# Landing x in three parts in another order: columns 0 to 511 of each row block first, the rest of both together

## What is computed

```python
h = rmsnorm(x, g_mix)                      # per row over 1024 columns
proj = einsum('bsd,de->bse', h, w_in)      # 1024 -> 4256
qa, ka, va, cq, ckv, kr, gate_a, gate_b = split(proj)
# rope, two attentions (8 heads each) over 256 rows, up-projections of cq and ckv
x = x + einsum(g_a * (o_a @ w_o_a) + g_b * (o_b @ w_o_b), w_out)
u = relu(rmsnorm(x, g_mlp) @ w_ff1)        # 1024 -> 4096
x = x + (u * u) @ w_ff2                    # 4096 -> 1024
return rmsnorm(x, g_final)
```

## Time and profile before

| | us |
|---|---|
| median of 3 runs | 364.59 |
| lowest, highest | 364.46, 365.83 |
| the profiled execution's own time | 364.77 |
| its span (first to last instruction) | 363.0 |

### The profile page before, as it was taken

The page is one execution under the profiler, slowest core; times in us unless marked ns, Lnnn a source line. Parts: engine busy times, 40 slices in busy tenths (PEclk is TensorE's granted clock), DMA queues, the critical chain, the costliest instruction groups (busy, mean ns, idle before and its releaser), DMA issues.

```text
span 363.0 us, 5565 instructions
## 1 busy us (share of the span) xinstructions
PE 356.1 (98%) x2109; PEld 310.9 (86%) x2109; DVE 287.4 (79%) x404; ACT 231.8 (64%) x384; POOL 40.9 (11%) x62
## 2 busy tenths in 40 slices
PE   8999999999999999999999999999999999999993
PEld 7998889887788888888888899999999999999983
DVE  4877973958877777487587879999998888998584
ACT  5996436987565675064466657777677777665424
POOL 1341000000000100000021011111101111220002
PEclk9999999999999999999999999999999999999999
DMA  8999567665341366328165999999999998963003
GB/s 263 382 388 311 221 187 239 214 225 166 134 142 38 106 233 228 116 89 325 51 212 168 273 334 221 279 301 293 287 267 268 278 280 248 294 171 116 2 0 116
DMA packets 42198, 76.77 MB, mean 212 GB/s; under 512 B 1924, under 2 KB 19345, under 8 KB 41921
## 3 DMA queue, kind: packets, MB, share of 16 engines
q1 hardware_dynamic: 37840, 66.59, 53.6%
q0 software_dynamic: 4176, 9.64, 13.4%
q10 hardware_dynamic: 160, 0.27, 0.2%
HBM read 75.44 MB, written 1.05 MB: 211 GB/s over the span
## 4 chain that ended last, share of the span: by engine, by line
PE 96%; DMA 1%; DVE 1%; ACT 0%; issue 0%; POOLq 0%; DVEq 0%; SPq 0%; POOL 0%; ACTq 0%
PE ps L1413 29%; PE ps L1415 29%; PE ps L1414 29%; PE ps L1420 4%; PE ps L1611 2%; PE ps L1636 2%; DMA raw<-in_w_in_dram 1%; ACT prob L560 0%; PE ps L1498 0%; PE ps L1527 0%; PE ps L1522 0%; PE ps L1532 0%; DVE xs L1172 0%; POOLq L129 0%; DVE qkT_b L1403 0%
## 5 line engine op out<-in xcount | busy, mean ns | idle before, releaser
L544 ACT ACTIVATE whi<-raw 128x1024 fp32r<-128x1024 f32 (+3 forms) x127 | 119.6, 989 | 14.7 <-PE ps L1415 13.4
L944 DVE TENSOR_TENSOR wlo<-raw,whi 128x1024 fp32r<-128x1024 f32 (+2 forms) x64 | 69.9, 1127 | 25.4 <-ACT whi L544 25.3
L1413 PE MATMUL ps<-whi,xT_hi 128*128 128x512 f32 (+2 forms) x188 | 73.4, 390 | 0.0
L1415 PE MATMUL ps<-whi,xT_lo 128*128 128x512 f32 (+2 forms) x188 | 71.3, 379 | 0.0
L1414 PE MATMUL ps<-wlo,xT_hi 128*128 128x512 f32 (+2 forms) x188 | 71.2, 378 | 0.0
L1415 PE MATMUL ps<-xT_hi,wlo 128*128 128x256 f32 x224 | 63.4, 283 | 0.0
L1414 PE MATMUL ps<-xT_lo,whi 128*128 128x256 f32 x224 | 63.4, 283 | 0.0
L1413 PE MATMUL ps<-xT_hi,whi 128*128 128x256 f32 x224 | 63.3, 283 | 0.0
L1413 PE MATMUL ps<-whi,lat_hi 128*128 128x512 f32 (+2 forms) x134 | 51.7, 385 | 0.0
L1414 PE MATMUL ps<-wlo,lat_hi 128*128 128x512 f32 (+2 forms) x134 | 51.2, 382 | 0.0
L1415 PE MATMUL ps<-whi,lat_lo 128*128 128x512 f32 (+2 forms) x134 | 51.1, 382 | 0.0
(11 more groups left out here) (157 smaller groups left out, 499.9 us busy)
## 6 DMA issues: line engine op xcount, KB each, us to landing
raw<-in_w_ff_dram SPq DMA_DIRECT2D x32, 1024.0 KB, 7.2
raw<-in_w_in_dram SPq DMA_DIRECT2D x14, 1024.0 KB, 6.3
raw<-in_w_out_dram SPq DMA_DIRECT2D x4, 1024.0 KB, 5.1
t_raw<-in_w_ff_dram SPq DMA_DIRECT2D x12, 256.0 KB, 7.9
raw<-in_w_ff_dram POOLq DMA_DIRECT2D x12, 256.0 KB, 4.8
t_raw<-in_w_ff_dram POOLq DMA_DIRECT2D x12, 256.0 KB, 7.2
gates<-in_b_gate_dram POOLq DMA_DIRECT2D x2, 1024.0 KB, 6.8
raw<-in_w_o_a_dram SPq DMA_DIRECT2D x2, 1024.0 KB, 5.1
```

What stands on the lines that cost most here:

```text
L544: return nc.scalar.activation(dst, src, ACT.Copy, scale=scale)
L944: nc.vector.tensor_tensor(wlo[:, s, h * w:(h + 1) * w], raw[:, s, h * w:(h + 1) * w], whi[:, s, h * w:(h + 1) * w].bitcast(F32), ALU.subtr ...
L1413: nc.tensor.matmul(dst, a_hi, b_hi, start=start, stop=False)
L1415: return nc.tensor.matmul(dst, a_lo, b_hi, start=False, stop=stop)
```

## The change

Three things are changed. Part 0 of x is row block 0's columns 0 to 511 (256 KB) and no longer all of that block (512 KB). Part 1 is row block 1's columns 0 to 511 as before, and part 2 is columns 512 to 1023 of both row blocks in one load (512 KB), where it was row block 1's alone. SP issues the parts at the same places of its queue. TensorE's eight transpositions of tiles 4 to 7 all stand behind the wait for part 2, in pairs (0, k), (1, k), and `first_rows(1, 0)` and `first_rows(1, 1)` stand ahead of that wait instead of behind it. The products of zeros at the start are 18 and 5 in number, not 22 and 7.

```diff
-WARM_UP = (22, 7)
+WARM_UP = (18, 5)
 REWARM = 4
-X_PARTS = ((0, 0, KT), (1, 0, 4), (1, 4, KT))
+X_PARTS = ((0, 1, 0, 4), (1, 2, 0, 4), (0, 2, 4, KT))
...
             def load_x(i):
-                t, cols = X_PARTS[i][0], slice(X_PARTS[i][1] * P, X_PARTS[i][2] * P)
-                sp.dma_start(xs[:, t, cols], x_v[:, t, cols]).then_inc(x_landed[i], 16)
+                t0, t1, k0, k1 = X_PARTS[i]
+                cols = slice(k0 * P, k1 * P)
+                sp.dma_start(xs[:, t0:t1, cols], x_v[:, t0:t1, cols]).then_inc(x_landed[i], 16)
...
             for k in range(4):
                 turn_x(0, k).then_inc(x_turned, 1)
-            turn_x(0, 4)
-            turn_x(0, 5)
...
             x_lows(2)
-            turn_x(0, 6)
-            turn_x(0, 7)
             w_lows(2)
...
             x_lows(3)
             w_lows(3)
+            first_rows(1, 0)
+            first_rows(1, 1)
             pe.wait_ge(x_landed[2], 16)
             for k in range(4, KT):
+                turn_x(0, k)
                 turn_x(1, k).then_inc(x_turned, 1)
-            for k in range(4):
-                first_rows(1, k)
+            first_rows(1, 2)
+            first_rows(1, 3)
             for k in range(4, KT):
                 pe.wait_ge(xT_lo_done, len(TURNED) + k - 3)
                 proj(CQ, k)
```

## The result

| | before | with the change |
|---|---|---|
| median | 364.57 us (18 runs, 364.21 to 365.88) | 365.68 us (18 runs, 365.30 to 366.20) |
| ratio | 1 | 1.0029, 95% interval 1.0021 to 1.0036 |
| profiled execution: time, span | 364.77, 363.0 us | 365.85, 364.0 us |
| k tile 4 of the first projection starts | 11.77 us | 12.74 us |

The kernel is 1.06 us slower by the ratio (0.77 to 1.31): clear of noise, and inside the 0.5% that the prediction called no change. Its time, 365.68, lies in the stated range (363.8 to 365.7) by 0.02 us, and outside the 364.3 to 365.0 that the prediction held likeliest.

What follows compares the result with a forecast made beforehand. TensorE, busy 98% of the span, bounds the kernel, with loads ahead of its gapless stream. Landings -0.70, moved turns +0.44, gap +0.35 make +0.09, a late chain +0.16 in all: 364.59 to 364.75 us, range 363.8 to 365.7.

Steps and rivals of the forecast that it cites:

- the sum of +0.16 us: Start of k tile 4: TensorE's own sum +0.09 us, but tile 4's chain ends 0.08 later, +0.16 in all.
- what the prediction gave 0.60: The main forecast for the whole kernel: 364.3 to 365.0 us around 364.75, chance 0.60.
- Its own sign of being wrong: Start of the first 288-column matmul, forecast 16.1 us; over 16.5 either the landings or the clock are wrong.
- 262 KB less ahead, so landings 0.70 us sooner: Head of the load queue: part 0, weight tiles and part 1 land about 0.70 us sooner, part 2 as before.
- The moved transpositions, +0.44: Turns (0,4) to (0,7) behind part 2 stand in a gapless TensorE stream: 4 x 0.11 = +0.44 us.
- The gap of 0.35 us ahead of the second row block's first product: TensorE idles 0.35 us awaiting row block 1 tile 0's low part, a wait the four turns filled before.
- What is late next: Chain from turn (1,4) at 10.04 through high part, weight copy and low part releases tile 4's matmul at 11.93.
- The residue of 0.08 us: At k tile 4, the wait for weight 4's low part ends 0.08 us behind TensorE's own sum.
- 18 and 5 products: Six fewer products of zeros at the start: worth nothing alone, since weight tile 0's load hides it.
- The landings stay: Rival: slow loads at the start are tied to time, not data; +0.45 to +0.86 us, 365.0 to 365.45, chance 0.15.
- Half clock: Rival: TensorE stays at 1.2 GHz beyond the wait for part 2; +2.0 us, 366.6, chance 0.05.
- The gain arrives: Rival: weights land still earlier or the 0.35 us gap is absent; 364.1 us, chance 0.20.

Runs made afterwards that it cites:

- e1: Kernel before with only the products of zeros changed, 18 and 5 in place of 22 and 7: 364.59 us, +0.11 (-0.36 to 0.58).
- e4: Changed kernel with the three loads of x as before, so TensorE's order and 18 and 5 products alone: 366.20 us, +1.75 against before (1.17 to 2.33).
- e7: Kernel before with only transpositions (0,4) to (0,7) moved behind the wait for the last part of x: 364.85 us, +0.55 (0.22 to 0.88).
- e8: Kernel before with only first_rows(1, 0) and (1, 1) moved ahead of the wait for the last part of x: 365.56 us, +1.17 (0.77 to 1.60).
- e2: Changed kernel with 22 and 7 products of zeros as before: 365.80 us, +1.28 against the kernel before (0.84 to 1.68).
- e3: Changed kernel with all four first_rows behind the eight transpositions: 366.13 us, +1.60 against the kernel before (1.02 to 2.19).
- E9: Kernel before with part 0 of x loaded as two half rows back to back, weights behind both: 364.93 us in one run.
- e11: Kernel before with part 0 of x loaded as two half rows back to back, timed over several runs: 365.32 us, +0.87 (0.51 to 1.24).
- e6: Kernel before with SP waiting for the masks before its first load, so all loads come 1.58 us later: 366.79 us in one run.

## Why the prediction was right, and where it was wrong

It forecast no change that a measurement tells, at 364.75 and up to 365.7. The time is 365.68, and the ratio's interval lies wholly above 1. That it falls in the range at all is luck: the sum of +0.16 us was off by 0.9, and what the prediction gave 0.60 did not happen. Its own sign of being wrong came true: the first matmul of 288 columns stands at 17.01, over the 16.5 from which "either the landings or the clock are" wrong. It was the landings.

*262 KB less ahead, so landings 0.70 us sooner.* This is the step that failed. It held for part 0 (0.7) and weight tiles 0 and 1 (0.5 each: 2.9 and 3.6 us from issue, 3.4 and 4.1 before), and for nothing behind them: tile 2 came 4.66 us after its issue, where the earlier trace rows have 4.6. And part 2, which I left in place because the bytes ahead of its end are the same, came 0.7 later. Several profiles say the same (us from issue to landing, issues at the same times):

| loads | tile 0 | tile 1 | tile 2 | tile 3 | part 1 | part 2 |
|---|---|---|---|---|---|---|
| as before (before, e1, e4, e7, e8) | 3.4 to 3.5 | 3.7 to 4.1 | 3.8 to 4.6 | 3.9 to 4.7 | 4.2 to 4.9 | 4.4 to 5.1 |
| of the change (change, e2, e3) | 2.9 | 3.5 to 3.6 | 3.6 to 4.7 | 4.7 to 4.8 | 4.9 to 5.0 | 5.8 to 6.5 |

The first transposition of row block 1 stands at 7.92 to 8.43 in the first five and at 8.35 to 8.41 in the other three, where the prediction had 7.73. Nor was tile 2 what the stretch up to 8 us waited for in the kernel before: the chain shows 0.06 us there.

Why, is argued and not shown. I had counted bytes and not how they are cut. The table of runs orders by it: with 512 KB of x in half rows 335 to 346 GB/s (five profiles), with 1024 KB 291 to 321 (six), with none 348 (one, hardly more than 346). The change doubles the half rows, at the head of the queue. The three profiles with its loads have as many loads as before, issued at the same times, so there the pace is lower without a further load; but they also have another order of bytes. E9 and e11 keep the order and add a load. The cut itself is cheap in a usual packet: at the start of every trace that has them, a packet of half a row of x took 84 ns at the median, and one of a whole row 159. The rest is in slow packets, of up to 1.9 us (e2). Whether they go with the size of the pieces, the places in memory that they skip, the order or the further load, no run here separates.

The prediction also prices the half at 0.60 us by a fit. The Trainium skill, DMA: Bandwidth & Descriptors, Anatomy of one DMA, states that fit for loads that GpSimd issues. These are issued by SP.

*The moved transpositions, +0.44.* Right: e7 measures +0.55 (0.22 to 0.88).

*The gap of 0.35 us ahead of the second row block's first product.* Right in place and size. TensorE had nothing between 9.19, when w_lows gives way (9.02 + 0.17), and 9.52: 0.33 us.

*What is late next.* Right: the chain from turn (1,4) ends last. I priced it at 1.89 us (10.04 to 11.93) and it took 1.93. It came 0.77 late as a whole, since its beginning at 10.04 counted on landings that were not sooner. The residue of 0.08 us by which it ends behind TensorE's own sum was 0.12. What I missed is that it, and not the gap, prices first_rows ahead of the wait: 0.35 by the gap, +1.17 (0.77 to 1.60) measured in e8.

*The terms don't add, and need not.* From the start of the fourth w_lows to k tile 4 the profiles have 2.73 us before, 3.15 in e7, 3.59 in e8, 3.70 in e4 and 3.72 in the change: +0.42, +0.86, +0.97 and +0.99. Both edits together cost 0.97 and not 1.28. In e8 TensorE waits at the end of the chain. In e4 and the change the moved turns fill that wait, and only the one ahead of turn (1,4) delays the chain, by its 0.11. By the medians e7 and e8 give 0.55 + 1.17 = 1.72 and e4 1.75, but e4's median lies between two groups of runs, and the intervals are too wide to tell. So the change loses what its order costs, 0.99, and gains nothing at the landings. Whether the sooner first load gives back a little is open.

*18 and 5 products.* Right: worth nothing that these runs tell (e1, up to 0.58; e2).

*The rivals.* "The landings stay" was priced at +0.45 to +0.86 and given 0.15. It is what happened, by its place in the chain. Its price was short by 0.1: by the profiles the change is 0.97 slower, 0.07 for a turn (1,4) still later than 10.04 + 0.70, and 0.04 for the chain. Its reason is doubtful: I had put slow loads down to the time since launch, and e6 speaks rather against that. "Half clock" was right in what it said of the level, and its price didn't come. With the change the four transpositions from 3.72 us start 0.21 us apart, twice the 0.11 of the earlier trace rows, so TensorE was at 1.2 GHz there, having run 18 and 5 products since 0.98 us, while the granted clock reads 1.00. The Trainium skill, TensorE: Matmul & The Clock Gate, What's actually happening, says that the warming takes an amount of time and not a number of products. The trace of the change, at the lower level as late as that, agrees as far as it goes; and the number alone indeed doesn't fix it: with 22 and 7 products from the same 0.98 us, six transpositions took 0.82 us in the kernel before and 1.49 in e8. In the change the price was nil, as weight tile 2 was the later. In the profiles of e1 and e6 the lower level was on the path. "The gain arrives" fell.

## What to carry to other kernels

Measure a smaller first load by the landings behind it, not by its bytes alone: here the third weight tile landed no sooner, and that took back what the shorter first load gave. Before moving work of the full engine to a later landing, follow the chain that starts from that work (here transposition, high part, weight, low part: 1.9 us) and count how much other work is left to cover it; an instruction put ahead of such a chain's first link delays the end by up to its own length, as far as nothing covers it (here six matmuls of 1.05 us in all, +0.86 by the profiles). And a filler that stands in a wait is free only there.

## What the runs showed of the hardware that was not expected

- The queue's pace from 2 to 10 us went with how much of x was loaded as half rows of 2 KB: 335 to 346 GB/s with half of x, 291 to 321 with all. The cause is not shown.
- TensorE at 1.2 GHz until 6.7 us cost nothing that the timing tells (e1: +0.11, -0.36 to 0.58), though it was on the path in that profile. At that level until 9.7 us it cost some 0.43 us (e6, one run).
- It rose at another moment in each profile: six transpositions took 0.82, 1.49 or 1.54 us. Up to 3.7 us the kernel before (0.82) and e8 (1.49) had run the same instructions at the same times.
